# A 31-tap depthwise convolution on TensorE: from split fp32r over two phases to plain fp32 over four

## The reference

```python
h = x @ w_pw1 + b_pw1
a, g = jnp.split(h, 2, axis=-1)
h = a * jax.nn.sigmoid(g)
h = causal_depthwise_conv(h, w_dw) + b_dw      # 31 taps, each channel by itself
h = jax.nn.silu(layer_norm(h, ln_g, ln_b))
return h @ w_pw2
```

## Time and profile before

| | |
|---|---|
| median of three runs | 2538.86 us |
| the profiled execution, its own time | 2539.48 us |
| its span in the profile | 2537.7 us |
| TensorE busy | 2515.6 us, 99% |
| VectorE busy | 1955.7 us, 77% |
| ScalarE busy | 1201.1 us, 47% |

### The profile page before, as it was taken

How to read it: one execution, slowest core, us unless ns; L and a number is a source line. 1 busy time by engine, 2 the same in 40 slices (tenths; PEclk the granted TensorE clock), 3 DMA queues, 4 the chain that set the end, 5 groups by cost and what they waited for, 6 DMA issues and landing times. The chain is left out here.

```text
span 2537.7 us, 41266 instructions
## 1 busy us (share of the span) xinstructions
PE 2515.6 (99%) x17241; PEld 2312.0 (91%) x17241; DVE 1955.7 (77%) x2571; ACT 1201.1 (47%) x1960; POOL 1.4 (0%) x10
## 2 busy tenths in 40 slices
PE   9999999999999999999999999999999999999999
PEld 7899999889888899998898899998898999999888
DVE  6989999578454679995784479996677979999576
ACT  6766444436233254443362254444356766444335
POOL 0000000000000000000000000000000000000000
PEclk9999999999999999999999999999999999999999
DMA  5203333324232233333233224333222203333322
GB/s 157 74 11 100 108 108 101 108 83 133 92 99 84 84 92 101 108 105 104 83 100 100 92 66 125 101 108 108 92 92 93 67 26 100 101 109 101 108 82 77
DMA packets 267054, 240.10 MB, mean 95 GB/s; under 512 B 14908, under 2 KB 212852, under 8 KB 266740
## 3 DMA queue, kind: packets, MB, share of 16 engines
q1 hardware_dynamic: 266292, 236.94, 30.1%
q10 hardware_dynamic: 576, 0.52, 0.1%
HBM read 233.21 MB, written 2.10 MB: 93 GB/s over the span
## 5 line engine op out<-in xcount | busy, mean ns | idle before, releaser
L1786 DVE TENSOR_TENSOR w_lo<-raw,w_hi 128x1024 fp32r<-128x1024 f32 x287 | 345.2, 1221 | 265.1 <-ACT w_hi L1309 264.6
L1309 ACT CAST w_hi<-raw 128x1024 fp32r<-128x1024 f32 x287 | 294.9, 1046 | 375.2 <-DMA raw<-in_ffn_w_down_dram 106.4
L879 PE MATMUL psum<-h_hi,w_lo 128*128 128x512 f32 x872 | 341.4, 392 | 0.0
L881 PE MATMUL psum<-h_hi,w_hi 128*128 128x512 f32 x872 | 339.3, 389 | 0.0
L880 PE MATMUL psum<-h_lo,w_hi 128*128 128x512 f32 x856 | 333.2, 389 | 0.0
L1024 PE MATMUL psum<-a_hi,w_lo 128*128 128x256 f32 x1088 | 280.0, 285 | 5.2 <-DVE w_lo L1786 3.6
L1024 PE MATMUL psum<-a_hi,w_hi 128*128 128x256 f32 x1088 | 276.6, 283 | 0.0
L1190 PE MATMUL psum<-h_hi,w_hi 128*128 128x256 f32 x768 | 217.3, 283 | 0.0
L1191 PE MATMUL psum<-h_hi,w_hi 128*128 128x256 f32 x768 | 217.3, 283 | 0.0
L1024 PEld LDWEIGHTS psum<-a_hi,w_lo 128*128 128x128 f32 x1088 | 208.6, 192 | 7.4 <-issue 3.7
L1321 ACT CAST w_hi<-w_hi_f 128x1024 fp32r<-128x1024 f32 x96 | 101.0, 1052 | 230.1 <-DVE w_hi_f L1814 230.1
(11 more groups left out here) (362 smaller groups left out, 6490.4 us busy)
## 6 DMA issues: line engine op xcount, KB each, us to landing
raw<-in_ffn_w_gate_dram SPq DMA_DIRECT2D x176, 256.0 KB, 3.0
raw<-in_ffn_w_up_dram SPq DMA_DIRECT2D x176, 256.0 KB, 3.4
raw<-in_ffn_w_down_dram SPq DMA_DIRECT2D x176, 256.0 KB, 3.2
raw<-in_a_w_pw_dram SPq DMA_DIRECT2D x94, 256.0 KB, 3.1
raw<-in_ple_w_gate_dram SPq DMA_DIRECT2D x64, 256.0 KB, 3.3
raw<-in_b_w_in_dram SPq DMA_DIRECT2D x64, 256.0 KB, 3.0
raw<-in_c_w_in_dram SPq DMA_DIRECT2D x48, 256.0 KB, 2.9
raw<-in_b_w_out_dram SPq DMA_DIRECT2D x32, 256.0 KB, 3.1
```

Of the source, the lines that this page charges most:

```text
L879: pe.matmul(bank(grp.g, j), st_lo, mv_hi, start=(k == 0), stop=False, skip_group_check=by_tiles(grp))
L881: done = pe.matmul(bank(grp.g, j), st_hi, mv_hi, start=False, stop=(ku == last and a == UK - 1), skip_group_check=by_tiles(grp))
L1309: act.copy(hi_u[u % RING], raw_u[u % RING]).then_inc(hi_ready, 1)
L1786: dve.tensor_tensor(lo_u[u % RING], raw_u[u % RING], hi_u[u % RING].bitcast(F32), ALU.subtract)\
```

## The change

TensorE now makes six tiles (2 to 7), all as plain fp32 with no hi and lo. Tiles 2 to 6 (`QUADS`, segments 0 to 4) go over four phases: four groups of 32 rows, blocks of 32 x 128 with four neighbouring taps, 128 moving columns, 34 steps a tile, each step four matmuls, one for each row group and each into a bank of its own. Tile 7 goes over two phases in two halves (segments 5 and 6): 32 steps of two matmuls each a half, 128 moving columns. Tile 2 begins on TensorE at tap 12, that is 22 steps; its first twelve taps are DVE's (`first_taps`), in two sums that are added later. Tiles 0 and 1 stay with DVE.

The blocks are made by DVE in one broadcast multiplication a tile with two small memsets for the zero edges (`make_blocks`), and ACT copies `conv_x` by phase once a tile (`conv_by_phase`). When a segment is through, its banks are moved out by small copies of 32 partitions x 128 (64 x 128 for tile 7) straight to the right partitions: 16 a tile, half of them "high" and half "low", on ACT or DVE. Segment i waits for both moves of segment i - 2. The DMAs and the hi and lo splits go.

```diff
+PHASES = 4
+STEPS = TAPS_A + PHASES - 1
+QUADS = (2, 3, 4, 5, 6, 7)
+PAIR_STEPS = TAPS_A + 1
+SEGMENT = P
+VECTOR_TAPS = 12
+SEGMENTS = ((0, None), (1, None), (2, None), (3, None), (4, None), (5, 0), (5, 1))
+CENTRE_IN, CENTRE_AT = 3, 14
+STATS_AT = 12
...
+        def moves(s, i, high):
+            n, h = SEGMENTS[i]
+            n_q, size, at = n_phases(n), P // n_phases(n), SEGMENT * (h or 0)
+            y = by_phase(tiles(h_f32, CONV_Y + QUADS[n]), n_q)
+            return [(y[r * size:(r + 1) * size, n_q - 1 - j, at:at + SEGMENT],
+                     segment_bank(s, i, r)[j * size:(j + 1) * size])
+                    for r in range(n_q // 2 * high, n_q // 2 * (high + 1)) for j in range(n_q)]
...
-                        if s.kind == "mixer_out" and s.layer % 3 == 0 and grp.index == 1 and ku == AHEAD:
-                            for n in range(len(PHASED)):
-                                turn_phases(s, n)
...
+            def quad_tap(s, i, e):
+                n = SEGMENTS[i][0]
+                for r in range(PHASES):
+                    moving = rows(conv_phases(n), r)[:, e % PHASES, e // PHASES:e // PHASES + SEGMENT]
+                    block = rows(tap_blocks(n), r)[:, e * ROWS:e * ROWS + P]
+                    last = pe.matmul(segment_bank(s, i, r), block, moving, start=(e == (VECTOR_TAPS if n == 0 else 0)), stop=(e == STEPS - 1))
+                return last
...
+                for i, (n, h) in enumerate(SEGMENTS):
+                    if i < 2:
+                        take_half(s.taps_g + i)
+                    else:
+                        pe.wait_ge(moved_high, moved(s, i - 2))
+                        pe.wait_ge(moved_low, moved(s, i - 2))
+                    if i == CENTRE_IN + 1:
+                        pe.wait_ge(centre_saved, c + 1)
+                    pe.wait_ge(conv_phased, len(QUADS) * c + n + 1)
+                    pe.wait_ge(blocks_made, len(QUADS) * c + n + 1)
+                    for e in range(VECTOR_TAPS if n == 0 else 0, STEPS if h is None else PAIR_STEPS):
+                        last = quad_tap(s, i, e) if h is None else pair_tap(s, i, e)
+                        if i == CENTRE_IN and e == CENTRE_AT:
                             centre(s)
+                        if i == LAST and e == STATS_AT:
+                            conv_stats(s, 0)
...
                         act.wait_ge(pe_done, s.groups[-1].end())
+                        conv_by_phase(s, 4)
+                        conv_by_phase(s, 5)
                         split_more(AHEAD)
+                        for i in range(2):
+                            move(s, i, 1)
+                            move(s, i, 0)
+                        move(s, 2, 0)
                         save_centre(s)
...
+                load_silu()
+                move(s, LAST, 1)
+                half_affine_pair(s, 0, 0)
...
                         convolve(s, 0, *w, 0, 10, TAPS_A, "a_b_dw", lo_end_at=ahead)
+                        make_blocks(s, 0)
+                        make_blocks(s, 1)
                         gated_input(s, s.groups[1])
...
                         convolve(s, 0, *w, 21, 24, TAPS_A, "a_b_dw", fresh=False, lo_end_at=ahead)
-                        conv_lo(s, 0)
-                        conv_lo(s, 1)
+                        make_blocks(s, 2)
                         lo_more()
                         convolve(s, 0, *w, 24, TAPS_A, TAPS_A, "a_b_dw", fresh=False, lo_end_at=ahead)
-                        own.settle()
-                        convolve(s, 2, *w, 0, 4, TAPS_A, "a_b_dw", lo_end_at=ahead)
+                        make_blocks(s, 3)
                         gated_input(s, s.groups[3])
...
+                        make_blocks(s, 4)
+                        make_blocks(s, 5)
                         lo_to(ahead)
                         lo_more(AHEAD)
-                        convolve_alone(s, 2, K_SHARED, TAPS_A)
-                        phase_add(s, 2)
-                        norm_centre_sum(y)
+                        first_taps(s, QUADS[0])
+                        centre_sum(s)
```

More of the change, by code:

```diff
@@ L916, in centre @@
             def centre(s):
+                pe.wait_ge(moved_low, moved(s, CENTRE_IN - 1))
                 pe.wait_ge(ysum_ready, s.layer // 3 + 1)
-                pe.matmul(bank(s.taps_g + 1, 0), ones_r[:, :], ysum[:, :], start=True, stop=True).then_inc(centre_done, 1)
+                for h in range(2):
+                    last = pe.matmul(mean_bank(s)[:, h], ones_r[:, :], hcol(ysum, h), start=True, stop=True)
+                last.then_inc(centre_done, 1)
             def conv_stats(s, h):
+                pe.wait_ge(moved_high, moved(s, LAST - 1 + h))
                 pe.wait_ge(conv_sums, 4 * (s.layer // 3) + 2 * h + 1)
@@ L950, in conv_taps, with pair_tap @@
+            def pair_tap(s, i, e):
+                n, at = SEGMENTS[i][0], e // 2 + SEGMENT * SEGMENTS[i][1]
+                for r in range(2):
+                    own = slice(r * PAIR_ROWS, (r + 1) * PAIR_ROWS)
+                    last = pe.matmul(segment_bank(s, i, r), tap_blocks(n)[own, e * PAIR_ROWS:e * PAIR_ROWS + P],
+                                     conv_phases(n)[own, e % 2, at:at + SEGMENT], start=(e == 0), stop=(e == PAIR_STEPS - 1))
+                return last
             def conv_taps(s):
-                c, n_diags, n_diag = s.layer // 3, 2 * (len(PHASED) - 1) + len(LAST_PARTS), 0
+                c = s.layer // 3
@@ L1422, in save_centre, with move @@
+            def move(s, i, high):
+                act.wait_ge(taps_done, moved(s, i))
+                for y, out_of in moves(s, i, high):
+                    last = act.copy(y, out_of)
+                last.then_inc(moved_high if high else moved_low, 1)
             def save_centre(s):
                 act.wait_ge(centre_done, s.layer // 3 + 1)
-                act.activation(mean[:, :], bank(s.taps_g + 1, 0), ACT.Copy, scale=2.0).then_inc(centre_saved, 1)
+                act.activation(mean[:, :].rearrange("p (h s) -> p h s", h=2), mean_bank(s), ACT.Copy, scale=2.0)\
+                    .then_inc(centre_saved, 1)
@@ new lines, in move, with first_taps @@
+            def move(s, i, high):
+                dve.wait_ge(taps_done, moved(s, i))
+                for y, out_of in moves(s, i, high):
+                    last = dve.tensor_copy(y, out_of)
+                last.then_inc(moved_high if high else moved_low, 1)
+            def first_taps(s, m):
+                for k in range(VECTOR_TAPS):
+                    own.settle(back=1)
+                    x, w, y = conv_x[:, m, k:k + SEQ], col("a_w_dw", s.layer // 3 * TAPS_A + k, m), tiles(tmp, 4 + k % 2)
+                    if k < 2:
+                        own.add(dve.tensor_scalar(y, x, w, None, ALU.mult))
+                    else:
+                        own.add(dve.scalar_tensor_tensor(y, x, w, y, ALU.mult, ALU.add))
@@ L2253, in convolve @@
                         lo_to(min(lo_end[0] + 1, lo_end_at))
-                    for m in (m0, m0 + 1) if k > first or not begun else ():
+                    for m in (m0, m0 + 1):
                         x = conv_x[:, m, PAD - taps + 1 + k:PAD - taps + 1 + k + SEQ]
@@ L2375, in epilogue @@
                     own.add(dve.memset(conv_x[:, :, 0:PAD], 0.0))
+                    own.add(dve.memset(conv_x[:, :, PAD + SEQ:CW], 0.0))
                 if s.kind == "short_in":
```

500 lines of the change are left out of this document (179 added, 321 removed).

## The result

The median went from 2538.74 to **2518.59 us** (four runs each; after 2516.00 to 2520.14, before 2538.58 to 2539.81). The ratio is 0.9919 with a 95% interval of 0.9902 to 0.9936, that is 20.2 us less; the forecast was 2519 us. Measured again later, the two kernels gave 2517.27 and 2539.89 us, a ratio of 0.9911 (0.9896 to 0.9926).

The account below looks back on a forecast made before the run. TensorE bounds the kernel: taps 52.4, centre 0.64 and statistics 1.2 make 54.2 us, with exit 1.5 a 55.7 us stage, 9.9 and 10.1 less. 2539.48 - 20.0 = 2519.5, so 2519 us; range 2512 to 2540.

Parts of the forecast that it names:

- The forecast's case: Both stages of taps on TensorE: four row groups run side by side, 20.0 us less together, 2519 us; chance 0.64.
- the signs that were named: TensorE's timeline: four 32-row matmuls together every 0.11 us; stages 55 to 56 us; no idle at segments 1, 2, 6.
- The step: TensorE's taps: 0.236 us a step, between 0.222 and 0.89; 158 + 64 steps make 52.4 us a layer.
- The statistics: Statistics matmuls in the stage: 0.99 us before, 1.2 us now, since the array goes to 128 rows and back.
- Later moves are shared with DVE and have 3 us or more: Bank moves after segment 2's low half, by ACT and DVE: 3 us or more to spare.
- The copies: ACT's moves out of the banks: 16 copies of 128 columns at 0.29 us, 4.7 us a tile.
- the rival in which the moves set the pace: ACT's moves at 0.6 us a copy lose some 5 us a layer: 2529 us, chance 0.11.
- The bound that was named: Start of segment 2: it would wait for ACT's moves if a copy took over 0.48 us instead of 0.29.
- DVE ahead of the centre: DVE's work before segment 3's centre: ready with `ysum` at 122.0 us, wanted at 125.0, 3 us to spare.
- The exit: Last tap to next product: ACT's two "high" block moves turn 1.06 us into 1.5; bounds 1.06 and 2.5.
- The rule that was held against the change: At `quad_tap`: matmuls start in strict program order and only weight loads are pulled ahead; it gave the slower case.
- the rival built on it: At `quad_tap`: second records hold up the next row group, 0.46 us a step, 2590 us; chance one in five.

Follow-up runs that it names:

- eight-step kernel: The changed kernel with eight steps (16 records) of one row group behind each other in TensorE's stream before the next group's turn; 2856.71 us.
- one record a matmul: The changed kernel with tiles 2 to 6 rounded to fp32r, low parts left out: 2520.70 us; with four steps of a row group behind each other 2521.03 us.
- doubled copies: The changed kernel with each of segment 0's 16 copies made once more by ACT into unused words, ahead of the real one; 2532.61 us.

## Why the prediction was right, and where its steps were off

The forecast's case came true: the row groups work side by side, and of the signs that were named the starts in fours are there. Its total is within half a microsecond, but that is luck: errors cancel, and for the profiled execution, for which the sum gives 2519.5 us, 2516.0 were measured. A layer's stage was to take 55.7 us and took 55.93 and 54.58. Against the named signs TensorE is idle in segment 6, ahead of the statistics.

- **The step.** Taken as 0.236 us between bounds of 0.222 and 0.89; it is 0.223 for four row groups and for two, the lower bound. 222 steps take 49.5 us and not 52.4: 2.9 us a layer too much in the sum. The value came from pairs of fp32r matmuls with 256 columns; the plain fp32 rows of the full array would have given it exactly.
- **The statistics.** Two plain fp32 matmuls took 149.92 - 148.88 = 1.04 us, for 1.2. (The 0.2 us on either side of the centre, from which the 1.2 came, is read too high: of the 0.64 us there some 0.12 are a pair and, by an estimate from the 0.23 us between 512-column matmuls of `conv_in`, 0.23 the centre itself, so some 0.3 are left for both sides.) But they wait 0.85 and 0.89 us for DVE's sum. For DVE's work behind segment 3 nothing was laid out; it was passed over with "Later moves are shared with DVE and have 3 us or more". This step of the prediction failed: all 16 copies of segment 4 stand in a row on ACT while DVE waits, and half of them moved to DVE took the wait away.
- **The copies.** Sized at 0.29 us from operations of 128 partitions that write `a_hi` in SBUF; the copies take 0.40 on ACT, and 0.40 on DVE too (8 in 3.19 us). The spare time before segment 2 is 0.2 us and not 2.8. The total didn't feel it, since 0.2 is still above nothing; the rival in which the moves set the pace was much nearer than its chance of 0.11 says. The bound that was named (a wait from 0.48 us a copy) was too generous: it is at 0.41.
- **DVE ahead of the centre.** `gated_input` of group 3 ended at 101.97 (102.7 foreseen), `ysum` began at 120.77 and was ready by 121.5 (122.0), the centre came at 125.09 (125.0): right. With 20 taps this cover is gone, and TensorE waits 3.1 us for `ysum`.
- **The exit.** 1.5 us foreseen, 1.63 measured. The cause is right in part: with the moves behind the Silu it shrinks to 1.41, not to the 1.1 that was expected of that trial, and then DVE's copies end it.
- **Not foreseen.** About 1 us a layer is gained at the second half's statistics. About 1.3 us is lost in layer 0, whose stage is longer than layer 3's by so much: segments 2, 3 and 4 are 0.88, 0.35 and 0.14 us longer, with the "issue" stalls of 0.36 and 0.30 us in the first two. They stood in the repeated run too, in layer 0 alone and at other places. In the kernels with two and three steps in a row the two layers' stages are as long as each other (54.93 and 54.85, 88.19 and 88.19 us). No experiment here was made for the cause: it is open.

The rule that was held against the change (the Trainium skill, TensorE: Matmul & The Clock Gate, Part 3: matmuls start in strict program order) does not hold across row groups as it stands: in the kernel after, row group 0's second record begins 0.19 us behind row group 3's first, and in the eight-step kernel a whole matmul does so: row group 0's last begins at 101.688, behind row group 1's first at 101.470, ahead of which it stands in the stream. But the rival built on it was not empty. With three steps a row group in a row, a step costs 0.446 us and the kernel 2584 us, nearly the 0.46 and 2590 us of that case. The change alternates row groups every two records, where the look ahead reaches (as it does with four); from six records up it doesn't. For what the Trainium skill says in TensorEngine Tiling (Array Packing), Tiling Modes, that different tiles load and multiply in parallel, the trace agrees for four row groups: 0.223 us for four matmuls, as for one of the full array.

## What to carry to other kernels

Price a step by its slowest row group's records, at the distance that dense records of the same type and columns have in the trace, and write the stream so that the row groups alternate every few records: here two or four in a row cost nothing, six doubled the step, and eight and more halved the clock as well. When TensorE gets faster, price the small work that empties its banks by rows of the same form (partitions, source in PSUM), since its spare time is the next bound. Look for a stretch in which one engine makes all of a job while the next consumer stands idle: half of it moved over was worth about a microsecond a layer (2517.27 to 2514.89 us).

## What the runs showed of the hardware that was not expected

- A matmul may begin before earlier ones of another row group, but only when three records or fewer of the group before are left to start; it held with one record a matmul and with two.
- The granted clock fell from 1.00 to 0.50 in a stream in which TensorE was busy 100% of the time, 3 to 6 us after the start of a stage in which three of a row group's 8, 16, 44 or 68 records overlap the next row group's; with three steps in a row, where three of six overlap, it stayed at 1.00 for the whole 70 us. That the overlap is the cause is argued from these four kernels.
- It also fell to 0.50 in or behind waits of TensorE: for 6.8 us at the wait of 6 us that the doubled copies made, for 3.4 us behind the wait of 3.1 us with 20 taps.
- A copy from PSUM of 32 partitions by 128 elements takes 0.40 us on ScalarE and on VectorE alike, those of segments 0 to 4 with every fourth word as their target. Those of 64 partitions by 128 with every second word stand with 267 ns in the mean on ScalarE, against 385. What makes the difference was not tried.
